# Moved work between waits, and a half-tile shift made by two on-chip transfers, in a three-pass fp32 layer kernel

## The chip, the cores and the metric

The kernel runs on one core of one Trainium2 chip. The metric is the device time of one execution in microseconds; the time before is the median of three runs. Engines are named as the hardware has them: TensorE (PE in the profile), VectorE (DVE), ScalarE (ACT), GpSimd (POOL), and SyncE (SP), which here only issues transfers.

## The reference, cut to what matters

One encoder layer on 1024 tokens of width 1024, in float32: a normalised input goes through one projection (1024 to 2304) whose columns feed three groups, their normalised outputs go through one output projection, and a squared-ReLU MLP of hidden width 4096 follows. The group that matters here is the chunked attention: four query heads, two key and value heads of 64, chunks of 64 tokens, and each chunk of queries reads its own chunk of keys and the one before.

```
def sliding_window_sink_attention(q, k, v, sinks, bias_band):
    ...
    def band(t):
        tc = t.reshape(B, nC, CHUNK, SWA_KV_HEADS, Dh)
        parts = [jnp.pad(tc, ((0, 0), (shift, 0), (0, 0), (0, 0), (0, 0)))[:, :nC]
                 for shift in reversed(range(WINDOW_CHUNKS))]
        return jnp.concatenate(parts, axis=2)
    kb, vb = band(k), band(v)
    ...
    o = jnp.einsum('bhgcqk,bckhd->bcqhgd', w.astype(vb.dtype), vb)
```

The two other groups are a stick-breaking attention (four heads of 64, strictly causal over all keys) and a recurrent block of width 512: a causal convolution over four tokens, two gates from small block-diagonal products, and a linear scan over the tokens, times a GeLU gate.

## The kernel before, in words

Every large product is made of three matmuls: both operands are split into a rounded high part and the rest (`w_hi`, `w_lo`, `act_hi`, `act_lo`), ScalarE writes the high part and VectorE the low one, and `three_passes` (L746, L748, L750) adds high times high, low times high and high times low in PSUM. Each engine has one program, written out in order; semaphores tie them together, and the order of the work is fixed by hand.

**Input projection.** The columns of `w_in` come in nine granules of 256 (`IN_COLS`), g = 0 to 8. SyncE's `load_in(g)` loads a granule as two halves into `stage` (L517); a half waits until VectorE has made the low part of the half that lay in `stage` before. ScalarE's `split_hi` rounds it (L1164), VectorE's `split_lo` subtracts (L1677). TensorE's `feature_major(g, n, half)` is one block of 24 matmuls, k = 0 to 7 with three passes each; blocks are counted as f = 4g + 2 half + n. Between blocks stand small pieces of work: after f = 4 `spread_norms` turns the token norms `rstd` into a row with eight transposes (L787), which ScalarE copies to `rs_row` and without which VectorE can copy no block out of PSUM; after f = 10, 16, 22 and 28 (`GATES_AFTER`) `gates(c)` makes the gate products of recurrent tile c (L819) once VectorE's `convolution(c)` is done (L1771). On `gates(c)` hang ScalarE's `recurrent(c)`, VectorE's `recurrent_input(c)` and `recurrent_scan(c)` (L1793 to L1798, which ends with `lru_done`), and after the last tile ScalarE's squares (L1305) and roundings (L1288) of the four recurrent tiles, VectorE's low parts of them (L1825), and then the softmax of the chunked attention.

**Chunked attention.** Four probability tiles h = 0 to 3. `window_scores(part)` (L847) makes scores for two tiles, VectorE's `window_max(h)` adds the bias and takes the maximum (L1870 to L1873), ScalarE's `window_exp(h)` follows (L1324), then VectorE's `window_norm(h)` (L1882), then TensorE's `window_turn(h)`, eight transposes (L911), then ScalarE's `window_copies(h)` (L1348). The values are turned token-major by `turn_cv` (L904), copied from PSUM to `cvtok` by ScalarE (L1317), and a second copy shifted by half a tile of 128 tokens, `cvshift`, is made by VectorE in `shift_v` (L1837 to L1840): the lower 64 partitions take the upper 64 of the tile before, the upper take the lower ones. `window_out(part, half)` (L939) reads `cvtok` for odd and `cvshift` for even chunks, and ScalarE's `window_output` copies it out (L1354).

**Around it.** `turn_v` transposes the values of the stick-breaking attention (L895), VectorE copies them to `vtok` (L1847); `recurrent_out(n)` is a row of twelve output-projection matmuls that needs nothing of the attentions; `scores(u)` (L958) are the stick-breaking scores, on which ScalarE's `weights` (L1366, L1370) wait, and of these `scores(1)` waits for the first two. TensorE's order before is

```
            window_turn(0)
            window_scores(1)
            window_turn(1)
            turn_cv()
            turn_v(0)
            window_out(0, 0)
            recurrent_out(0)
            window_out(0, 1)
            turn_v(1)
            scores(0)
```

ScalarE's order is `window_exp(0)`, `(1)`, `group_rsqrt(0)`, `window_copies(0)`, `(1)`, the copies to `cvtok`, `window_exp(2)`, `window_output(0, 0)`, `window_exp(3)`, `recurrent_row(0)`, `window_output(0, 1)`, `weights(0)`, `window_copies(2)`, `weights(1)`, `window_copies(3)`. VectorE's is `window_norm(1)`, `window_max(2)`, `group_rsqrt(0)`, `shift_v`, `window_max(3)`, `value_copies(0)`, `(1)`, `window_norm(2)`, `(3)`. SyncE issues, after the sink loads (L580), 16 small loads of gate weights (L586), then `load_in(2)` to `load_in(8)` and the output projection's granules; it issues in order and stops at each wait.

## Time and profile before

| | us |
|---|---|
| median of 3 runs (lowest, highest) | 1025.41 (1024.73, 1027.03) |
| the profiled execution, its own time | 1025.31 |
| its span, from first to last instruction | 1023.3 |
| TensorE busy in it | 1005.5 |
| VectorE, ScalarE, GpSimd busy | 796.3, 582.6, 90.8 |
| mean granted TensorE clock | 0.999 |

The span is what the profile shows; the run's time has about 2 us more around it. Starts and durations in the timeline are from the span's start. A wait is the idle time of an engine just before an instruction, put down to what ended it. After the first 350 us come the eight stages of the MLP, which the change does not touch.

### The profile page before, as it was taken

How to read it: one execution, taken by the hardware profiler on the slowest of the kernel's cores; microseconds unless marked ns; L12 is line 12 of the kernel's file. 1: busy time of each engine (PE TensorE's matmuls, PEld its weight loads, DVE VectorE, ACT ScalarE, POOL GpSimd, SP SyncE). 2: the span in 40 equal slices, each digit the busy share in tenths (PEclk: the TensorE clock that was granted, in tenths of full speed). 3: DMA queues.
4: the chain of work that ended last, by engine and by line, in shares of the span. 5: the costliest groups of instructions: out<-in, count | busy, mean ns of one | idle time of the engine just before them, and what ended most of it. 6: DMA issues, size and time to landing. Idle time of an engine off the chain costs nothing.

```text
span 1023.3 us, 12188 instructions
## 1 busy us (share of the span) xinstructions
PE 1005.5 (98%) x4846; PEld 812.4 (79%) x4846; DVE 796.3 (78%) x729; ACT 582.6 (57%) x760; POOL 90.8 (9%) x69
## 2 busy tenths in 40 slices
PE   9999999999999999999999999999999999999997
PEld 7878777877767788788888888888888888888884
DVE  6157759698787589967877777998777998778998
ACT  7424642759777547768653657333657333666455
POOL 0014213121322241000000000000000000000000
PEclk9999999999999999999999999999999999999999
DMA  9421111200101733021031031031031031035004
GB/s 331 138 83 42 42 42 42 83 1 1 42 2 42 265 126 144 1 103 63 1 114 51 1 121 45 1 123 42 1 124 42 1 124 42 1 124 206 0 1 165
DMA packets 38864, 74.64 MB, mean 73 GB/s; under 512 B 3444, under 2 KB 12952, under 8 KB 38808
## 3 DMA queue, kind: packets, MB, share of 16 engines
q1 hardware_dynamic: 38664, 73.83, 20.9%
q8 instruction: 39, 0.64, 0.3%
q14 instruction: 17, 0.14, 0.0%
q10 hardware_dynamic: 144, 0.03, 0.0%
HBM read 65.46 MB, written 8.39 MB: 72 GB/s over the span
## 4 chain that ended last, share of the span: by engine, by line
PE 86%; DVE 5%; ACT 3%; DMA 3%; SPq 2%; issue 1%; ACTq 0%; DVEq 0%
PE ps L746 26%; PE ps L750 26%; PE ps L748 26%; PE ps L983 2%; PE ps L911 2%; PE ps L958 2%; DMA xt<-in_x_turned 1%; DMA rel_row<-work 1%; SPq L586 1%; PE ps L819 1%; DVE y L2205 1%; DMA stage<-in_w_in 1%; PE ps L1058 1%; PE ps L828 1%; DVE out_gained L2143 0%
## 5 line engine op out<-in xcount | busy, mean ns | idle before, releaser
L746 PE MATMUL ps<-a_op,b_op 128*128 128x512 f32 x448 | 175.4, 392 | 2.5 <-issue 1.4
L750 PE MATMUL ps<-a_op,b_op 128*128 128x512 f32 x448 | 174.4, 389 | 0.0
L748 PE MATMUL ps<-a_op,b_op 128*128 128x512 f32 x448 | 174.3, 389 | 0.0
L746 PE MATMUL ps<-b_op,a_op 128*128 128x512 f32 x448 | 174.3, 389 | 0.0
L748 PE MATMUL ps<-b_op,a_op 128*128 128x512 f32 x448 | 174.3, 389 | 0.0
L750 PE MATMUL ps<-b_op,a_op 128*128 128x512 f32 x448 | 174.3, 389 | 0.0
L1524 ACT CAST a_op<-f 128x1024 fp32r<-128x1024 f32 x56 | 58.8, 1050 | 107.8 <-PE ps L750 77.7
L2049 DVE TENSOR_TENSOR b_op<-wq,b_op 128x1024 fp32r<-128x1024 f32 x96 | 117.0, 1219 | 0.0
L746 PE MATMUL ps<-act_hi,w_hi 128*128 128x512 f32 x288 | 113.6, 394 | 0.9 <-DVE w_lo L1677 0.7
L748 PE MATMUL ps<-act_lo,w_hi 128*128 128x512 f32 x288 | 112.1, 389 | 0.0
L750 PE MATMUL ps<-act_hi,w_lo 128*128 128x512 f32 x288 | 112.1, 389 | 0.0
L2038 DVE TENSOR_TENSOR a_op<-f,a_op 128x1024 fp32r<-128x1024 f32 x56 | 68.5, 1223 | 49.7 <-ACT a_op L1524 49.7
L1532 ACT CAST b_op<-wq 128x1024 fp32r<-128x1024 f32 x96 | 100.7, 1049 | 4.2 <-DVE y L1981 4.2
L746 PEld LDWEIGHTS ps<-a_op,b_op 128*128 128x128 f32 x448 | 84.1, 188 | 20.1 <-issue 1.8
L750 PEld LDWEIGHTS ps<-a_op,b_op 128*128 128x128 f32 x448 | 84.1, 188 | 17.6
L746 PEld LDWEIGHTS ps<-b_op,a_op 128*128 128x128 f32 x448 | 84.1, 188 | 17.5
L748 PEld LDWEIGHTS ps<-b_op,a_op 128*128 128x128 f32 x448 | 84.1, 188 | 17.5
L750 PEld LDWEIGHTS ps<-b_op,a_op 128*128 128x128 f32 x448 | 84.1, 188 | 17.4
L748 PEld LDWEIGHTS ps<-a_op,b_op 128*128 128x128 f32 x448 | 84.1, 188 | 17.0
L1524 ACT CAST a_op<-ut 128x1024 fp32r<-128x1024 f32 x32 | 33.6, 1052 | 74.4 <-PE ps L750 74.4
L746 PEld LDWEIGHTS ps<-act_hi,w_hi 128*128 128x128 f32 x288 | 54.2, 188 | 17.0 <-issue 3.4
L2092 DVE TENSOR_TENSOR y<-y,ps 128x1024 f32<-128x1024 f32 x54 | 63.1, 1215 | 0.0
(221 smaller groups left out, 1659.1 us busy)
## 6 DMA issues: line engine op xcount, KB each, us to landing
wq<-in_w_ff_in SPq DMA_DIRECT2D x16, 1024.0 KB, 5.4
wq<-in_w_ff_out SPq DMA_DIRECT2D x16, 1024.0 KB, 5.1
stage<-in_w_in SPq DMA_DIRECT2D x16, 512.0 KB, 4.0
y<-in_x SPq DMA_DIRECT2D x4, 1024.0 KB, 13.3
h_spill<-y SPq DMA_DIRECT2D x8, 512.0 KB, 2.7
h_back<-h_spill SPq DMA_DIRECT2D x2, 2048.0 KB, 12.0
out<-y SPq DMA_DIRECT2D x8, 512.0 KB, 3.2
stage<-in_w_out SPq DMA_DIRECT2D x6, 512.0 KB, 3.4
```

The costliest lines, as they stand in the source:

```text
L586: sp.dma_start(gate_w[r:r + HEAD, blk // 2, col:col + HEAD], w[0, blk])\
L746: nc.tensor.matmul(dst, stat[0], mov[0], start=first, stop=False, skip_group_check=chained)
L748: nc.tensor.matmul(dst, stat[0], mov[1], start=False, stop=False, skip_group_check=chained)
L750: return nc.tensor.matmul(dst, stat[1], mov[0], start=False, stop=last, skip_group_check=chained)
L911: mm = nc.tensor.transpose(ps[:, piece_bank(i), P * b:P * (b + 1)], c[:, P * b:P * (b + 1)], ident[:, :])
L958: mm = nc.tensor.matmul(ps[:, 2 * a + c, 0:cols.stop - cols.start], sq_t[p][rows, P * t:P * (t + 1)], sk_t[p][rows, cols], start=True, sto ...
L983: mm = nc.tensor.matmul(ps[HEAD * a:HEAD * (a + 1), 6, P * (t % 4):P * (t % 4 + 1)], vtok[:, j, P * p + HEAD * a:P * p + HEAD * (a + 1)], ...
L1524: nc.scalar.copy(a_op[:, (half + 2) % A_SLOTS, 0], src).then_inc(a_hi_ready, 1)
L1532: nc.scalar.copy(b_op[:, (half + 3) % B_SLOTS, 0], src).then_inc(b_hi_ready, 1)
L2038: nc.vector.tensor_tensor(slot[:, 1], a_source(*divmod(n, PRODUCTS), kk), slot[:, 0].bitcast(F32), ALU.subtract)\
L2049: nc.vector.tensor_tensor(slot[:, 1], src, slot[:, 0].bitcast(F32), ALU.subtract).then_inc(b_lo_ready, 1)
L2092: nc.vector.tensor_tensor(dst, dst, ps[:, bank:bank + 2, :], ALU.add)\
```

## The change

It has four parts. SyncE issues `load_in(2)` ahead of the 16 gate weight loads. TensorE's `spread_norms` moves from behind block 4 into block 5, after k = 2, and the last `gates` from behind block 28 into block 29, after k = 1. The two VectorE copies of `shift_v` become two transfers from `cvtok` to `cvshift` (229 KB and 262 KB, each to 64 partitions), issued by SyncE once `cvtok` is copied; VectorE keeps the memset of the first chunk, under a semaphore of its own. After `turn_cv` TensorE now goes to `recurrent_out(0)`, `window_out(0, 0)`, `turn_v(0)` in that order.

```diff
--- before.py
+++ after.py
@@ -240,8 +240,9 @@
         gelu_poly, gelu_sig, gelu_used = sem("gelu_poly"), sem("gelu_sig"), sem("gelu_used")
         decay_ready, one_minus, root_ready, lru_done = (
             sem("decay_ready"), sem("one_minus"), sem("root_ready"), sem("lru_done"))
-        v_turned, v_copied, cv_turned, cv_copied, cv_shifted = (
-            sem("v_turned"), sem("v_copied"), sem("cv_turned"), sem("cv_copied"), sem("cv_shifted"))
+        v_turned, v_copied, cv_turned, cv_copied, cv_shifted, cv_cleared = (
+            sem("v_turned"), sem("v_copied"), sem("cv_turned"), sem("cv_copied"),
+            sem("cv_shifted"), sem("cv_cleared"))
         win_scores, win_max, win_exp, win_probs = (
             sem("win_scores"), sem("win_max"), sem("win_exp"), sem("win_probs"))
         turned_ready, turned_copied = sem("turned_ready"), sem("turned_copied")
@@ -580,17 +581,22 @@
                 sp.dma_start(sink_c[HEAD * a:HEAD * (a + 1), kv:kv + 1],
                              swa_sinks[:, h:h + 1].partition_broadcast(HEAD))\
                     .then_inc(sinks_loaded, 16)
+            load_in(2, w_in[0], IN_COLS[2])
             for m, w in enumerate((lru_wa, lru_wx)):
                 for blk in range(2 * LRU_TILES):
                     r, col = HEAD * (blk % 2), HEAD * ((m + blk) % 2)
                     sp.dma_start(gate_w[r:r + HEAD, blk // 2, col:col + HEAD], w[0, blk])\
                         .then_inc(gate_w_loaded, 16)
 
-            for g in range(2, N_IN):
+            for g in range(3, N_IN):
                 load_in(g, w_in[0], IN_COLS[g])
 
             for n in range(2):
                 load_out(N_IN + n, w_out[0], (2 * P, 4 * P), 512 * n)
+            sp.wait_ge(cv_copied, 2)
+            sp.dma_start(cvshift[0:CHUNK, 1:TOK, :], cvtok[CHUNK:P, 0:TOK - 1, :])\
+                .then_inc(cv_shifted, 16)
+            sp.dma_start(cvshift[CHUNK:P, :, :], cvtok[0:CHUNK, :, :]).then_inc(cv_shifted, 16)
             load_out_by_group(N_IN + 2, w_out[0], 0)
             load_out_by_group(N_IN + 3, w_out[0], 512)
 
@@ -767,7 +773,7 @@
                         if k == KD - 1:
                             mm.then_inc(proj_ready, 1)
 
-            def feature_major(g, n, half):
+            def feature_major(g, n, half, between={}):
 
                 whi, wlo = w_slot(w_hi, g % 2, "in"), w_slot(w_lo, g % 2, "in")
                 for k in range(KD):
@@ -777,6 +783,8 @@
                                       (whi[:, k, cols], wlo[:, k, cols]),
                                       (act_hi[:, k, toks], act_lo[:, k, toks]),
                                       k == 0, k == KD - 1)
+                    if k in between:
+                        between[k]()
                 mm.then_inc(proj_ready, 1)
 
             def spread_norms():
@@ -868,15 +876,18 @@
                             pe.wait_ge(rs_row_ready, 1)
                         elif f >= 8:
                             pe.wait_ge(proj_copied, f - 7 if g == 2 else f - 3)
-                        feature_major(g, n, half)
-                        if f == 4:
-                            spread_norms()
+                        if f == 5:
+                            feature_major(g, n, half, {2: spread_norms})
+                        elif f == GATES_AFTER[-1] + 1:
+                            feature_major(g, n, half, {1: lambda: gates(LRU_TILES - 1)})
+                        else:
+                            feature_major(g, n, half)
                         if f == 8:
                             pe.wait_ge(proj_copied, 8)
                             pe.wait_ge(rel_back, 16)
                             nc.tensor.matmul(ps[:, 5, :], flip, work[0:CHUNK, 2, 0:4 * P],
                                              start=True, stop=True).then_inc(band_ready, 1)
-                        if 4 * g + 2 * half + n in GATES_AFTER:
+                        if 4 * g + 2 * half + n in GATES_AFTER[:-1]:
                             gates(GATES_AFTER.index(4 * g + 2 * half + n))
                         if f == 4 * N_IN - 4:
                             window_scores(0)
@@ -926,7 +937,8 @@
                 n = 2 * part + half
                 pe.wait_ge(turned_copied, win_piece(2 * part + 1, half) + 1)
                 if n == 0:
-                    pe.wait_ge(cv_shifted, 3)
+                    pe.wait_ge(cv_shifted, 32)
+                    pe.wait_ge(cv_cleared, 1)
                     pe.wait_ge(turned_copied, 4)
                 else:
                     pe.wait_ge(win_copied, n)
@@ -1011,9 +1023,9 @@
             window_scores(1)
             window_turn(1)
             turn_cv()
+            recurrent_out(0)
+            window_out(0, 0)
             turn_v(0)
-            window_out(0, 0)
-            recurrent_out(0)
             window_out(0, 1)
             turn_v(1)
             scores(0)
@@ -1834,11 +1846,7 @@
             def shift_v():
 
                 dve.wait_ge(cv_copied, 2)
-                nc.vector.memset(cvshift[0:CHUNK, 0, :], 0.0).then_inc(cv_shifted, 1)
-                nc.vector.tensor_copy(cvshift[0:CHUNK, 1:TOK, :], cvtok[CHUNK:P, 0:TOK - 1, :])\
-                    .then_inc(cv_shifted, 1)
-                nc.vector.tensor_copy(cvshift[CHUNK:P, :, :], cvtok[0:CHUNK, :, :])\
-                    .then_inc(cv_shifted, 1)
+                nc.vector.memset(cvshift[0:CHUNK, 0, :], 0.0).then_inc(cv_cleared, 1)
 
 
             def value_copies(part):
```

## Rows read from the trace of the kernel before

**Rows 1.** The page: the span, and the engines' busy time.
```profile
span 1023.3 us, 12188 instructions
...
PE 1005.5 (98%) x4846; PEld 812.4 (79%) x4846; DVE 796.3 (78%) x729; ACT 582.6 (57%) x760; POOL 90.8 (9%) x69
```

**Rows 2.** TensorE's waits, whole span: total us, times, longest us.
```profile
PE ps L895 <- ACT cvtok L1317: 1.2, 1, 1.2
...
PE ps L939 <- issue: 0.8, 1, 0.8
...
PE ps L746 <- DVE w_lo L1677: 0.7, 1, 0.7
PE ps L958 <- ACT sb_w L1370: 0.6, 1, 0.6
...
PE ps L787 <- DVE rstd L1692: 0.3, 1, 0.3
```

**Rows 3.** Timeline, 33 to 56 us: start us, us, what [idle before].
```profile
38.53 2.48 DVE L1807 SCALAR_TENSOR_TENSOR xr<-ps,rs_row 128x512 f32<-128x512 f32 x4 [2.34 <-ACT rs_row L1202]
...
40.10 5.07 SPq L586 DMA_DIRECT2D work<-in_lru_wx  x8
...
45.22 9.50 SPq L517 DMA_DIRECT2D stage<-in_w_in  x4
...
53.10 1.22 DVE L1677 TENSOR_TENSOR w_lo<-stage,w_hi 128x1024 fp32r<-128x1024 f32 x1 [1.47 <-ACT w_hi L1164]
```

**Rows 4.** Timelines by engine, 176 to 222 us.
```profile
177.15 1.99 PE L819 MATMUL ps<-work 64*128 64x512 f32 x8 [0.53 <-DVE work L1771]
...
195.72 2.01 ACT L1164 CAST w_hi<-stage 128x1024 fp32r<-128x1024 f32 x2 [3.73 <-PE ps L750]
...
196.12 1.22 DVE L1798 TENSOR_TENSOR xr<-xr,work 128x1024 f32<-128x1024 f32 x1
...
197.63 3.90 ACT L1305 ACTIVATE work<-xr 128x1024 f32<-128x1024 f32 x4
...
204.11 9.17 DVE L1825 SCALAR_TENSOR_TENSOR f_lo<-xr,columns_c,f_hi 128x1024 fp32r<-128x1024 f32 x4 [2.25 <-ACT f_hi L1288]
...
221.49 0.86 PEld L911 LDWEIGHTS ps<-ident,work 128*128 128x128 f32 x8 [0.41 <-DVE work L1882]
```

**Rows 5.** Timelines by engine, 226 to 237 us.
```profile
226.51 1.07 ACT L1317 COPY cvtok<-ps 128x512 f32<-128x512 f32 x2 [0.24 <-PE ps L904]
...
230.59 0.50 PE L746 MATMUL ps<-w_hi,f_hi 128*128 128x512 f32 x1
...
230.75 0.56 ACT L1354 COPY work<-ps 128x512 f32<-128x512 f32 x1
...
233.53 0.44 PE L939 MATMUL ps<-work,cvshift 128*64 128x128 f32 x4
...
235.69 1.29 DVE L1847 COPY vtok<-ps 128x512 f32<-128x512 f32 x2 [2.26 <-PE ps L895]
```

**Rows 6.** The chain that ended last, in order of time: start us, us, what.
```profile
228.12 0.62 DVE cvshift L1838
...
229.49 1.24 DVE sb_w L1870
...
232.27 1.22 ACT sb_w L1324 x6
...
242.91 1.77 PE ps L958 x8
```

**Rows 7.** Kinds of DMA issues: count, KB each, median us from issue to landing.
```profile
h_spill<-y SPq DMA_DIRECT2D x8, 512.0 KB, 2.7
...
stage<-in_w_out SPq DMA_DIRECT2D x4, 256.0 KB, 4.6
...
work<-in_lru_wa SPq DMA_DIRECT2D x8, 16.0 KB, 2.1
```

**Rows 8.** GB/s of all queues, 40 slices of 0.2 us from 322 us.
```profile
GB/s 0 0 0 102 123 133 317 369 410 389 430 297 72 215 154 143 246 266 348 358 287 287 195 72 41 20 20 20 10 0 0 0 0 0 0 0 0 0 0 0
```

## The prediction

> **What bounds the kernel now.** I read the page first. TensorE is busy for 1005.5 of 1023.3 us [rows 1], so nothing that only makes another engine shorter can pay; what can pay is TensorE's idle time, 17.8 us in all, some of it ahead of its first instruction and behind its last. The second view is the list of TensorE's waits. The ones that this change aims at are 0.7 us for the low half of the third weight granule, 0.3 us for the token norms, 1.2 us for `cvtok`, 0.8 us for `cvshift`, and 0.6 us for ScalarE ahead of `scores(1)` [rows 2]; a sixth, 0.53 us for the convolution ahead of the last `gates`, stands in [rows 4]. Together 4.1 us, 0.4% of the span: that is the most the change could bring if every wait went and none came back. So I followed each wait back in the timeline and in the chain that ended last, to see who is late next.
>
> **The third granule's load, moved ahead of the 16 gate weight loads: 0.7 us removed.** SyncE spends 0.63 us on each of them (5.07 for 8), the last ends at 45.2, and only then `load_in(2)` is issued; the low half of its second half runs from 53.10 to 54.32, and TensorE, which waits for it, starts 0.7 us late [rows 3, 2]. Issued 10.2 us earlier, the load is no longer the last thing: VectorE turns to it after four copies that end at 41.0 [rows 3], or near 43 with the next edit, still some 10 us ahead of TensorE. Its own waits are for granule 1's low halves, which TensorE reads already. Behind it the gate weights land 10.2 + 2.1 [rows 7] after their first issue, near 48, and the first `gates` comes three blocks after 54.3. What is queued behind on SyncE, `load_in(3)`, then waits for a low half that comes earlier too. Gain 0.7.
>
> **`spread_norms`, three k steps into the next block: 0.3 us removed.** The eight transposes start 0.29 us late, behind `rstd` [rows 2]. Nine matmuls of some 0.24 us (twelve stand between 230.59 and 233.53 [rows 5]) now lie ahead, so they start near 38 in place of 36.2. `rs_row` then comes at 40.2, and the next block that needs it starts near 42: covered. VectorE's four copies [rows 3] go from 38.5 to 40.3, with the slack just named. Gain 0.3; together 0.99 us with the granule.
>
> **The last `gates`, two k steps into block 29.** It waited 0.53 us [rows 4]. Six matmuls, 1.4 us, now go ahead of it. The convolution hangs by VectorE's and ScalarE's work on the `gates` before, so it comes 0.99 earlier; TensorE reaches `gates(3)` at 176.62 - 0.99 + 1.4 = 177.0, only 0.12 earlier than before (177.15), though TensorE itself is now 1.5 ahead. What hangs on `gates(3)` is a chain that TensorE doesn't enter: the sigmoids, the root, the scan, `lru_done` at 197.34, ScalarE's four squares at 197.63, its four roundings, VectorE's four low halves from 204.11 with no gap up to the first softmax, and at its end `window_turn(0)` at 221.5, whose weight load already waits on VectorE for 0.41 us [rows 4]. Before, the squares were held to 197.63 by ScalarE's `split_hi` ahead of them, which TensorE releases; that one now ends 1.5 earlier and `lru_done` (197.34 - 0.12, plus 0.05) takes over at 197.27. So the chain arrives 0.36 us earlier, not 1.5: **TensorE gets a new wait of about 1.1 us at `window_turn(0)`**, and of 1.5 us removed upstream 0.36 are left. If that chain had slack I don't see, up to 1.1 more would be left; if the move of `gates` cost more, nothing.
>
> **TensorE's new order after `turn_cv`.** `turn_cv` ends just ahead of the `cvtok` copies of 226.51 [rows 5], after the change near 226.1. `recurrent_out(0)` needs only things that are there, takes 2.94 [rows 5] and ends near 229.0; it covers the 1.2 us wait for `cvtok`. Then comes `window_out(0, 0)`, ahead of `turn_v(0)`, and it waits for the shifted values.
>
> **The shift as two transfers.** VectorE loses two copies, 1.37 us from 228.12 to 229.49, which are on the chain that ended last: they delay `window_max(3)`, whose end releases `window_exp(3)` at 232.27; from there ScalarE runs without a gap up to `scores(1)` at 242.91 [rows 6]. After, `window_max(3)` ends near 232.27 - 0.36 - 1.37 = 230.5. But the shift now takes: `cvtok` copied at 227.58 - 0.36 = 227.22 [rows 5]; SyncE, which has nothing due behind that wait until the next two output granules, issues the first at 227.25 and the second 0.64 later (the 0.63 of [rows 3], whose transfers also fill 64 partitions); then the landing of 229 KB and 262 KB. No transfer from SBUF to SBUF is in the trace. From below, a 16 KB one lands in 2.1 us. A 512 KB store out of SBUF takes 2.7; two of 256 KB to 64 partitions each, issued back to back, take 4.6 [rows 7], with other data ahead of them and a source in HBM. The pair moved at 143 to 246 GB/s at first and at 358 at most, against the 430 just before [rows 8]. I take 3.3 for the second: the store's 2.7 and a third of the way to the pair, as this source is near and its lines are long, but the partitions are half. It lands at 227.9 + 3.3 = 231.2, and `window_out(0, 0)` starts at 231.3, after a wait of 2.3 us that takes the place of 1.2 + 0.8.
>
> The Trainium skill on the same term, which the sum does not use: the page SBUF — State Buffer (section on Door 1, the DMA port swizzle) says that 64 partitions of one half reach 8 of the 16 ports; at half of its 436 GB/s the two would need 2.25 us of data, and with the fixed 2.0 us of the page DMA: Bandwidth & Descriptors (section on the anatomy of one DMA) land some 4.3 after the first issue, an estimate that gives +1.0 us in place of +0.7; the slow start of the pair in [rows 8] agrees with it.
>
> **Who waits for that.** ScalarE's order is unchanged: `window_exp(2)`, then the output copy of `window_out(0, 0)`, then `window_exp(3)`. So the copy, which before started at 230.75 [rows 5], now starts at 231.3 + 1.1 and `window_exp(3)` 0.55 later, at 232.95, where before it started at 232.27: **0.7 us later, and with it the chain of [rows 6]**, weights(0), weights(1) and `scores(1)`. VectorE: `turn_v(0)` now ends at 233.4, the value copies follow it and `turn_v(1)`, and end near 237.0, as before (236.98 [rows 5]), so it adds nothing. TensorE behind that: `turn_v(0)`, `window_out(0, 1)`, `turn_v(1)`, `scores(0)` fit before 237.5. From 243 on all engines follow one another by work and not by the clock, and the shift stays.
>
> **The sum.** Upstream -0.36; from `cvtok` to `window_exp(3)` +1.04; net +0.7 on the profiled 1025.31 (span 1023.3 and 2.0 around it). That execution lies 0.1 below the median of 1025.41. On the median: 1026.1. Each 0.1 us in the landing is 0.1 us of the kernel; break-even is a second transfer that lands 2.6 us after its issue.
>
> **Rivals.** *The transfers are quick.* At 2.1 us [rows 7] the second lands at 230.0, the sum is -0.6: 1024.8. At 2.7 it is +0.1. For it: SyncE has no other transfer under way, and SBUF is at both ends. Against: two transfers share the engines, and both are issued at 0.63. By that DMA page of the Trainium skill, 2.0 us and the second transfer's bytes at 436 GB/s make 2.6: break-even; it is a fit for another issue path, so I give it no more. *The transfers are as slow as the pair of [rows 7]*, the case on the other side: at 4.6 us it lands at 232.5, `window_exp(3)` starts at 234.25, +2.0: 1027.4; from 4.7 us it is slower by over 0.2%. For it: the one row of its shape. Against: that pair ran behind a 512 KB load. *The gap fillers' gain comes through:* the chain behind `gates(3)` has slack, no new wait at `window_turn(0)`, and 1.1 more is saved: -0.4 with my landing, 1025.0, and -1.7 with the quickest. For it: the waits list shows no wait of TensorE there; against: the 0.41 us of its weight load. *The change does nothing:* the waits only change their names; that is my case to within 0.7.
>
> **How the numbers follow.** My case (landing 2.9 to 3.9 us, +0.3 to +1.3) 0.5; quick 0.22; slow 0.13; the gain comes through 0.1; others 0.05, such as a lower clock after the longer gap (it is 0.999 in the mean now, but no gap of TensorE in [rows 2] is as long as 2.3 us). The range takes in the quick case with the gain (-1.7) and the slow one (+2.0, or +2.4 with no gain upstream): 1023.8 to 1027.9; my case alone is 1025.7 to 1026.7. About 0.2%, 2.05 us, is what a measurement tells from no change. Faster by more needs the quick landing and the whole upstream gain and a little besides: 0.07. Slower by more is the upper part of the slow case and a clock that falls: 0.12. Same: 0.81.
>
> **What the profile after would show.** TensorE's waits for `w_lo` near 54, for `rstd` near 36, for the convolution at 177 and for `cvtok` are gone; a wait of about 1.1 us stands at L911's first transposes, for VectorE; one of about 2.3 us for DMA at `window_out`; `scores(1)` waits near 1.2 in place of 0.6. Two issues of 0.6 us stand on SyncE at 227.25, and the second lands near 231.2. The prediction is wrong if `window_turn(0)` starts well before 221, or if `window_exp(3)` starts before 232 or after 234.

## The result and the profile after

The changed kernel took 1027.25 us (median of 20 runs, 1025.67 to 1028.77), the kernel before 1025.39 us (20 runs, 1024.14 to 1027.88). The ratio is 1.0014, 95% interval 1.0008 to 1.0020: slower by some 1.4 us, inside the 0.2% within which the prediction counted a time as the same. (The two medians differ by 1.86 us, more than the ratio says; its interval reaches from 0.8 to 2.05 us.) On the median that the forecast of 1026.1 was made on, 1025.41, the ratio makes 1026.8, just above its likeliest case's own range.

The page of the changed kernel: span and TensorE's busy time, which answer to [rows 1].

```profile
span 1025.5 us, 12189 instructions
...
PE 1005.9 (98%) x4846; PEld 813.4 (79%) x4846; DVE 794.6 (77%) x727; ACT 582.3 (57%) x760; POOL 93.4 (9%) x69
```

The span is 2.2 us longer, TensorE's busy time 0.4: the rest is idle time. Its waits over the whole span (total us, times, longest us) answer to [rows 2]:

```profile
PE ps L951 <- issue: 2.6, 1, 2.6
PE ps L752 <- DVE act_lo L1732: 1.6, 1, 1.6
...
PE ps L922 <- DVE work L1890: 1.1, 1, 1.1
...
PE ps L970 <- ACT sb_w L1382: 0.8, 1, 0.8
```

The five waits that the change aimed at (`cvtok`, `cvshift`'s copies, `w_lo`, `rstd`, the convolution at 177) are gone. In their place stand two that were not there, 2.6 us at `window_out(0, 0)` (L951; "issue" means that nothing the profile shows ended it, here the transfers) and 1.1 us at `window_turn(0)` (L922, for the normalised tile), and 0.8 in place of 0.6 at `scores(1)` (L970). The wait for `act_lo` (1.6) belongs to the first input tiles; in a second profile of the unchanged kernel, below, it is 1.8.

Timelines by engine, 33 to 50 us, beside [rows 3]: start us, us, what, and in brackets the idle time before.

```profile
34.25 1.14 SPq L518 DMA_DIRECT2D stage<-in_w_in  x2
...
38.77 1.04 PE L795 MATMUL ps<-ident,rstd 128*128 128x128 f32 x8
...
43.41 2.35 DVE L1689 TENSOR_TENSOR w_lo<-stage,w_hi 128x1024 fp32r<-128x1024 f32 x2
```

`load_in(2)` is now issued at 34.25, ahead of the gate weights; `spread_norms` starts with no wait (38.77); VectorE turns to the granule's low halves at 43.41, more than 10 us ahead of TensorE.

Timelines by engine, 176 to 222 us, beside [rows 4]:

```profile
177.36 1.99 PE L827 MATMUL ps<-work 64*128 64x512 f32 x8
...
197.59 3.90 ACT L1317 ACTIVATE work<-xr 128x1024 f32<-128x1024 f32 x4 [1.02 <-DVE xr L1810]
...
221.48 1.09 PE L922 MATMUL ps<-ident,work 128*128 128x128 f32 x8 [1.13 <-DVE work L1890]
```

`gates(3)` (L827) has no bracket any more. But ScalarE's squares (L1317) wait 1.02 us, for VectorE's scan, and TensorE stands 1.13 us ahead of `window_turn(0)`.

Timelines by engine, 226 to 235 us, beside [rows 5]:

```profile
226.49 1.07 ACT L1329 COPY cvtok<-ps 128x512 f32<-128x512 f32 x2 [0.23 <-PE ps L915]
...
227.59 0.50 SPq L597 DMA_DIRECT2D cvshift<-cvtok  x1
228.14 0.60 SPq L599 DMA_DIRECT2D cvshift<-cvtok  x1
...
231.96 0.70 PE L951 MATMUL ps<-work,cvshift 128*64 128x128 f32 x4 [2.56 <-issue]
...
233.98 0.59 ACT L1366 COPY work<-ps 128x512 f32<-128x512 f32 x1 [3.14 <-PE ps L951]
234.46 0.40 ACT L1336 ACTIVATE sb_w<-sb_w,m_row 128x128 f32<-128x128 f32 x1
```

SyncE issues 0.03 us after the `cvtok` copies end (227.56); the second transfer is issued at 228.14; TensorE comes out of its wait at 231.96. The kinds of DMA issues say how long they took (count, KB, median us from issue to landing), for [rows 7]:

```profile
cvshift<-cvtok SPq DMA_DIRECT2D x1, 256.0 KB, 3.7
cvshift<-cvtok SPq DMA_DIRECT2D x1, 224.0 KB, 2.9
```

The second lands at 228.14 + 3.7 = 231.84. And the chain that ended last, in order of time (start us, us, what), for [rows 6]:

```profile
229.40 2.56 issue
231.96 1.99 PE ps L951 x16
...
233.98 0.59 ACT work L1366
234.56 1.11 ACT sb_w L1336 x6
...
245.09 1.77 PE ps L970 x8
```

`window_exp(3)` (L1336) starts at 234.46, where it started at 232.27, and `scores(1)` at 245.09, where it started at 242.91. The same delay of 2.2 us at both, and it is the 2.2 us of the span.

One thing is in no row of before: the clock. First one window of the kernel before, then those of the changed kernel from 228 us; the columns are the stretch, its length, the busy time and count of PE, PEld, DVE, ACT and POOL, the granted clock, the DMA share and GB/s.

```profile
232.00:234.00 2.00, 2.00 (x16) 1.45 (x16) 1.42 (x3) 1.73 (x9) 0.00 (x0) 1.00 0.00 0
```

```profile
228.00:232.00 4.00, 1.44 (x9) 0.87 (x8) 2.60 (x4) 2.83 (x15) 0.00 (x0) 0.98 0.48 125
232.00:234.00 2.00, 2.00 (x17) 1.67 (x18) 0.00 (x0) 0.02 (x1) 0.00 (x0) 0.50 0.00 0
234.00:236.00 2.00, 2.00 (x16) 1.84 (x18) 0.33 (x1) 2.00 (x9) 0.00 (x0) 0.68 0.00 0
236.00:238.00 2.00, 2.00 (x22) 1.56 (x20) 1.24 (x3) 2.00 (x12) 0.00 (x0) 1.00 0.03 8
```

TensorE's granted clock is 0.50 of full, the lower of its two levels, from 231.8 to 235.3: 3.3 us of it behind the gap. `window_out(0, 0)` took 1.99 us there (chain, 231.96), where the same sixteen matmuls take 1.09 at full clock (in the filled gap, below). In before's profile no microsecond from 0 to 1021 has a clock under 0.98.

### The profile page after: what moved, and what is told of

Its sections match the earlier page's. It is cut to its first block, busy times and chain, and to the rows that moved or that the text cites. A ratio compares the mean times of both kernels' runs of the same rounds, so it can differ in the third digit from the quotient of the medians.

```text
span 1025.5 us, 12189 instructions
## 1 busy us (share of the span) xinstructions
PE 1005.9 (98%) x4846; PEld 813.4 (79%) x4846; DVE 794.6 (77%) x727; ACT 582.3 (57%) x760; POOL 93.4 (9%) x69
## 4 chain that ended last, share of the span: by engine, by line
PE 89%; DVE 5%; ACT 3%; issue 1%; DMA 1%; SPq 0%; DVEq 0%; ACTq 0%
PE ps L752 27%; PE ps L756 27%; PE ps L754 27%; PE ps L922 2%; PE ps L995 2%; PE ps L970 2%; DVE f_lo L1837 1%; PE ps L827 1%; DVE y L2213 1%; DMA xt<-in_x_turned 1%; PE ps L1070 1%; DVE out_gained L2151 0%; PE ps L951 0%; ACT sb_w L1382 0%; ACT work L1317 0%
## 6 DMA issues: line engine op xcount, KB each, us to landing
y<-in_x SPq DMA_DIRECT2D x4, 1024.0 KB, 12.5
```

## The experiments

The kernel start differs from execution to execution: TensorE's wait for the first input tiles lasts between 0.2 and 1.8 us. So stretches of the profiles are compared by distances. In the table, *a* is from TensorE's relative-bias matmul (at 18.89 us in before's profile, before all that the change touches) to the first transposes of `window_turn(0)`; *b* from the start of ScalarE's `cvtok` copies to the start of `window_exp(3)`; *c* from the same to `scores(1)`; *d* from the relative-bias matmul to `scores(1)`. Each is a difference of two starts in one kernel's timelines; from `window_turn(0)` to the `cvtok` copies it is 5.01 or 5.02 us in every kernel here.

| kernel | a | b | c | d | median us | ratio to before, 95% |
|---|---|---|---|---|---|---|
| before | 202.61 | 5.76 | 16.40 | 224.02 | | |
| before, a second time | 201.11 | 5.76 | 17.75 | 223.87 | 1026.33 | 0.9999 (0.9989 to 1.0010) |
| changed | 201.64 | 7.97 | 18.60 | 225.25 | 1027.25 | 1.0014 (1.0008 to 1.0020) |
| changed, a second time | 201.62 | 7.96 | 18.59 | 225.23 | 1026.80 | 1.0005 (0.9994 to 1.0015) |
| load and norms alone | 201.10 | 5.77 | 16.40 | 222.51 | 1024.59 | 0.9991 (0.9979 to 1.0003) |
| gates back | 201.08 | 7.16 | 18.25 | 224.34 | 1026.09 | 1.0000 (0.9987 to 1.0013) |
| copies back | 201.64 | 5.77 | 16.40 | 223.05 | 1024.98 | 0.9994 (0.9981 to 1.0007) |
| copies and gates back | 201.09 | 5.76 | 16.40 | 222.51 | 1024.14 | 0.9985 (0.9976 to 0.9994) |
| `turn_v` first | 201.62 | 7.09 | 18.06 | 224.70 | 1026.54 | 1.0005 (0.9993 to 1.0018) |
| half size | 201.63 | 6.19 | 16.82 | 223.46 | 1025.28 | 0.9997 (0.9982 to 1.0013) |
| filled gap | 201.63 | 7.09 | 17.72 | 224.36 | 1026.39 | 1.0008 (0.9999 to 1.0017) |
| late copies | 201.09 | 4.25 | 16.16 | 222.26 | 1024.50 | 0.9985 (0.9977 to 0.9994) |
| exp first | 201.09 | 4.25 | 16.15 | 222.26 | 1024.00 | 0.9981 (0.9972 to 0.9990) |
| weights early | 201.07 | 4.25 | 15.38 | 221.46 | 1023.24 | 0.9970 (0.9959 to 0.9981) |

The kernels below the first row were timed in three sets, each beside its own executions of before (medians 1025.72, 1026.11 and 1026.03), and the ratio is to those; the row "changed" is the result above. So times of different sets are compared by their ratios.

The distances are steady to some 0.03 us where nothing differs between two kernels (the 201.07 to 201.10 of six profiles), the timed ratios only to some 0.1%; so the distances carry the small differences, and the times say whether the end agrees. Two limits: each distance is from one execution, and all end at `scores(1)`. What is left of the span from there is 780.3 to 780.5 us in nine of the profiles, and 781.2 to 782.9 in gates back, copies back, copies and gates back, late copies and weights early, which have a stretch at the lower clock between 276 and 284 us; no distance shows that.

**The last `gates` back behind block 28.** All else is as in the changed kernel.

```diff
-                        elif f == GATES_AFTER[-1] + 1:
-                            feature_major(g, n, half, {1: lambda: gates(LRU_TILES - 1)})
...
-                        if 4 * g + 2 * half + n in GATES_AFTER[:-1]:
+                        if 4 * g + 2 * half + n in GATES_AFTER:
```

> The changed kernel, with the last gates back behind block 28. Theory: the move of gates did not save its 0.5 us but handed it on with a surcharge, since what waits for it is the chain through VectorE and ScalarE up to window_turn(0). Then with the move undone a wait of about 0.5 us comes back ahead of the last gates, the wait of 1.1 us at window_turn(0) shrinks to 0.5 or less, and window_turn(0) starts about 0.6 us earlier, counted from the first block; the kernel is 0.6 us faster than the changed one, 1026.6. Rival: the move is worth what it removed; then it is 0.5 us slower, 1027.8, with the wait at window_turn(0) as long as before.

The waits of TensorE in this kernel:

```profile
PE ps L949 <- issue: 2.6, 1, 2.6
...
PE ps L827 <- DVE work L1781: 0.5, 1, 0.5
```

The wait for the convolution is back with 0.5 us, the one at `window_turn(0)` is gone from the list, and *a* is 0.56 shorter. So the move of the last `gates` costs 0.56 us: the wait that it removed came back twice as long behind it, since the chain that hangs on `gates(3)` runs on ScalarE and VectorE alone. The gap at `window_out(0, 0)` is as in the changed kernel, 2.6. But *b* is 7.16 and not 7.97: the clock fell later. The windows of this kernel:

```profile
230.00:232.00 2.00, 1.32 (x17) 1.11 (x18) 0.00 (x0) 0.12 (x1) 0.00 (x0) 0.89 0.00 0
232.00:234.00 2.00, 2.00 (x12) 1.67 (x13) 0.22 (x1) 2.00 (x10) 0.00 (x0) 0.50 0.00 0
```

TensorE came out of the gap at 230.68 and did `window_out(0, 0)` at full clock; the fall came at 231.5, and most of its price stands in *c* (18.25). The time, 1026.09 with a ratio of 1.0000, lies below the expected 1026.6, and its interval tells it neither from before nor from the changed kernel: that the move costs 0.56 us rests on *a* alone.

**VectorE's copies back.** The two transfers are taken out, the two copies put in again; TensorE keeps its new order.

```diff
-            sp.wait_ge(cv_copied, 2)
-            sp.dma_start(cvshift[0:CHUNK, 1:TOK, :], ...
-            sp.dma_start(cvshift[CHUNK:P, :, :], ...
...
+                nc.vector.tensor_copy(cvshift[0:CHUNK, 1:TOK, :], cvtok[CHUNK:P, 0:TOK - 1, :])\
+                    .then_inc(cv_shifted, 1)
+                nc.vector.tensor_copy(cvshift[CHUNK:P, :, :], cvtok[0:CHUNK, :, :])\
+                    .then_inc(cv_shifted, 1)
```

> The changed kernel, with the shift made by VectorE's two copies again; TensorE's new order and the gap fillers stay. Theory: the loss lies in the late landing and in the lower clock that follows the gap of 2.6 us ahead of window_out. Then window_out(0, 0) waits 0.1 us or nothing, the granted clock stays at 1.00 there, window_exp(3) starts 2.5 us earlier than with the transfers, and the kernel takes 1024.8, below both. Rival: the new order of TensorE costs by itself (the value copies and turn_v come late); then it stays above 1026.

TensorE's waits:

```profile
PE ps L966 <- ACT sb_w L1378: 1.3, 1, 1.3
PE ps L918 <- DVE work L1890: 1.1, 1, 1.1
```

The 2.6 us gap is gone, *b* is back at 5.77, 2.20 shorter where 2.5 was expected, and the time goes with it: 1024.98, ratio 0.9994, against 1.0014 and 1.0005 of the changed kernel's two rows (the intervals of this one and the second overlap). The 1.1 at `window_turn(0)` stays, so the two parts are independent. At `scores(1)` stand 1.3 us: TensorE has caught up there, and waits for ScalarE's `weights`, whose distance (*c*) is that of before to 0.01. The transfers, then, cost 2.2 us in the changed kernel's profile, the clock's fall included (7.97 - 5.77). Behind that wait, the clock fell here too: in the chain that ended last, `scores(1)` takes 3.13 us, and 1.77 in [rows 6].

```profile
242.30 3.13 PE ps L966 x8
```

**The load and the norms alone**, on the kernel before, with nothing else of the change.

```diff
+            load_in(2, w_in[0], IN_COLS[2])
             for m, w in enumerate((lru_wa, lru_wx)):
...
-            for g in range(2, N_IN):
+            for g in range(3, N_IN):
...
-                        feature_major(g, n, half)
-                        if f == 4:
-                            spread_norms()
+                        feature_major(g, n, half, {2: spread_norms} if f == 5 else {})
```

> The kernel before, with the third granule's load ahead of the gate weights and with spread_norms inside block 5, and nothing else. Theory: these two waits come off for good, since the chain up to window_turn(0) begins at a block of TensorE that comes earlier with them; TensorE's later waits stay as they were. Then it is 1.0 to 1.3 us faster than before: 1024.3. Rival: they are handed on to window_turn(0) as the move of gates was; then a wait of 1 us stands there and the time is that of before, 1025.4 to 1025.7.

*a* is 1.51 us shorter than in before's profile, and the two start alike (the relative-bias matmul at 18.89 and 18.81); *b* and *c* are those of before: the two gap fillers bring 1.51, not 0.99. The waits list shows the 0.7 and 0.3 us that TensorE stood; it does not show what else the stop cost (below).

**The copies and the gates back**, both of the edits above: what is left is the load, the norms and TensorE's new order.

> The changed kernel, with VectorE's copies and the last gates where they were; the load, the norms and TensorE's new order stay. Theory: both losses are taken back and the gains stay: against the kernel with only the copies back (1024.98) it wins what the gates cost, 0.6 to 1.1 us, so 1024.1; the waits of 2.6 us at window_out and of 1.1 us at window_turn(0) are both gone. Rival: the new order gives nothing beyond the load and the norms; then it equals the kernel that has only those two.

In every distance it is the kernel with the load and the norms alone. The new order of TensorE gives nothing by itself: it removes waits for `cvtok` and `cvshift` (1.2 and 0.8), but `scores(1)` hangs on ScalarE's `weights`, and *c* is ScalarE's: TensorE only waits there longer, 1.3 in place of 0.6.

**`turn_v(0)` ahead of `window_out(0, 0)`.** TensorE's order becomes `recurrent_out(0)`, `turn_v(0)`, `window_out(0, 0)`, `window_out(0, 1)`, `turn_v(1)`, `scores(0)`: 1 us of its work goes into the gap.

> The changed kernel, with turn_v(0) ahead of window_out(0, 0) again (after recurrent_out(0)): nothing is taken away, but 1.0 us of other work fills the gap. Theory that the clock fell because of the length of the gap: the gap shrinks from 2.6 to about 1.5 us, the clock stays at 1.00 as it did past the gap of 1.2 us, window_out(0, 0) takes 1.0 in place of 2.0 us, window_exp(3) starts 1.0 us earlier, and the kernel gains 1.0 to 1.5 us: 1026.0. Rival: the lower clock has another cause (the mean load of the stretch); then it falls again and the kernel stays at 1027.2.

TensorE's timeline and the windows of this kernel:

```profile
231.78 0.44 PE L951 MATMUL ps<-work,cvshift 128*64 128x128 f32 x4 [1.70 <-issue]
...
233.65 0.44 PE L951 MATMUL ps<-work,cvshift 128*64 128x128 f32 x4 [0.77 <-ACT work L1366]
```

```profile
232.00:234.00 2.00, 1.23 (x23) 1.02 (x21) 0.00 (x0) 1.08 (x4) 0.00 (x0) 1.00 0.00 0
234.00:236.00 2.00, 2.00 (x18) 1.67 (x15) 0.00 (x0) 2.00 (x11) 0.00 (x0) 0.51 0.03 8
```

The gap falls to 1.70, `window_out(0, 0)` does not start earlier (231.78), but it runs at full clock, and *b* is 7.09 in place of 7.97: 0.88 us of the delay in *b* is the clock, 1.33 the transfers. The expectation that a gap of this length leaves the clock alone failed: it fell 2 us later, behind a further 0.77, so that *c* is still 18.06, and the time is 1026.54 where 1026.0 was expected.

**Half the size.** Four transfers, tiles 0 to 3 first and, once they have landed, 4 to 7; `window_out(0, 0)` waits for the first pair, `window_out(1, 0)` for the second.

```diff
-            sp.dma_start(cvshift[0:CHUNK, 1:TOK, :], cvtok[CHUNK:P, 0:TOK - 1, :])\
+            sp.dma_start(cvshift[0:CHUNK, 1:4, :], cvtok[CHUNK:P, 0:3, :]).then_inc(cv_shifted, 16)
+            sp.dma_start(cvshift[CHUNK:P, 0:4, :], cvtok[0:CHUNK, 0:4, :]).then_inc(cv_shifted, 16)
+            sp.wait_ge(cv_shifted, 32)
...
+                    if n == 2:
+                        pe.wait_ge(cv_shifted, 64)
```

> The changed kernel, with the shift in two pairs of transfers: tiles 0 to 3 first, which the first two window_out read, and tiles 4 to 7 after them. Theory that the landing is fixed cost and data: with half the bytes the second transfer of the first pair lands 0.5 to 0.6 us sooner (3.1 in place of 3.7 us from its issue), the gap shrinks to 2.0 us, and window_exp(3) starts 0.5 us earlier, or 1.5 if the clock stays up: 1026.7 or 1025.8. Rival: the landing is fixed cost alone; then it lands as late and nothing changes, 1027.2.

The DMA issues and TensorE's timeline of this kernel:

```profile
cvshift<-cvtok SPq DMA_DIRECT2D x3, 128.0 KB, 2.3
...
cvshift<-cvtok SPq DMA_DIRECT2D x1, 96.0 KB, 2.3
```

```profile
230.35 0.44 PE L957 MATMUL ps<-work,cvshift 128*64 128x128 f32 x4 [1.70 <-issue]
```

The transfer that TensorE waits for, the second of the first pair, was issued at 227.42, and SyncE, which waits for the same landing, goes on at 230.28: it took 2.8 us, where the one of 256 KB took 3.7. The gap is 1.70, *b* 6.19. A landing that cost the same at any size is out, and one that is all data too: halving it takes 0.9 us off, where 0.5 to 0.6 was expected, and as much off *b* (7.09 at full clock to 6.19). The clock stayed up there, and the time is 1025.28, where 1025.8 was expected for that case.

**A filled gap.** Twenty transposes of the identity, whose results nothing reads, stand between `recurrent_out(0)` and `window_out(0, 0)`; TensorE's real work comes no earlier.

```diff
             recurrent_out(0)
+            pe.wait_ge(cv_copied, 2)
+            for i in range(20):
+                nc.tensor.transpose(ps[:, 4, P * (i % 4):P * (i % 4 + 1)], ident[:, :],
+                                    ident[:, :])
             window_out(0, 0)
```

> The changed kernel with work added, none taken away: 20 transposes of the identity into a free bank (their result is not used), behind recurrent_out(0), once cvtok is copied; they fill some 2.2 of the 2.6 us in which TensorE waits for the transfers. Theory: the lower clock past the gap is a price of its own, beside the late landing. Then the transfers land as before, the clock stays at 1.00 from 232 to 236 us, window_out(0, 0) takes 1.0 in place of 2.0 us, window_exp(3) starts 1.0 us earlier, and the kernel is 1.0 to 1.7 us faster than the changed one, near 1025.9. Rival: the two halved stretches cost nothing that is not hidden, or the clock falls anyway; then it stays at 1027.2.

TensorE's timeline and the windows:

```profile
229.16 2.35 PE L1029 MATMUL ps<-ident 128*128 128x128 f32 x20
231.88 0.44 PE L951 MATMUL ps<-work,cvshift 128*64 128x128 f32 x4 [0.38 <-issue]
```

```profile
232.00:234.00 2.00, 2.00 (x26) 1.66 (x27) 0.00 (x0) 0.99 (x4) 0.00 (x0) 1.00 0.00 0
```

The clock stays at 1.00, and *b* is 7.09, as with `turn_v(0)` first. `window_out(0, 0)` starts 5.48 us behind the start of the `cvtok` copies, as late as in the changed kernel (5.47), and takes 1.09 us in place of 1.99: this is what the lower clock costs where it covers that stretch. That filling the gap keeps the clock up is not shown by it: this is one profile, 5 of the 11 timed executions still have a mean clock under 0.998 (7 of the 11 of the changed kernel beside them), and the median is 1026.39 against 1026.80, where 1025.9 was expected.

**Late copies and exp first.** Two kernels with `gates` back, in which the orders give the shift time: ScalarE runs `window_exp(3)` ahead of `window_output(0, 0)`, and TensorE's order is `recurrent_out(0)`, `turn_v(0)`, `scores(0)`, `window_out(0, 0)`, `turn_v(1)`, `window_out(0, 1)`. The one makes the shift by VectorE's copies, behind `window_max(3)`; the other by the two transfers.

```diff
             window_exp(2)
-            window_output(0, 0)
             window_exp(3)
+            window_output(0, 0)
```

> As the one before, with three moves more: VectorE makes the copies behind window_max(3), ScalarE runs window_exp(3) ahead of the output copy of window_out(0, 0), and TensorE puts turn_v(0) and scores(0) ahead of window_out(0, 0) and turn_v(1) ahead of window_out(0, 1). Theory: window_max(3) and then window_exp(3) end the wait of that stretch; with the shift off that chain window_exp(3) starts 1.4 us earlier than in the one before, and about 1.3 us more is gained: 1022.9 to 1023.5. Rival: VectorE is the next to be late (value copies and two norms follow); then it gains under 0.3 us.

> As the one before in every order, but with the shift made by the two transfers. Theory: the transfers are as good as the copies, or better, once something covers them: turn_v(0) and scores(0) stand ahead of window_out(0, 0), so that the landing, 4.2 us after cvtok is copied, ends 1 us or more ahead of need; no gap over 1 us and a clock of 1.00 there; VectorE is 1.4 us freer than with its copies, and the time is that of the one before or up to 0.7 us under it, 1022.5 to 1023.3. Rival: a cost of the transfers that is not the wait (slower neighbours, a longer landing); then it is slower than the one before by 0.5 us or more.

TensorE's waits at `scores` in the kernel with the transfers:

```profile
PE ps L968 <- ACT sb_w L1380: 1.3, 1, 1.3
...
PE ps L968 <- DVE m_row L1879: 0.5, 1, 0.5
```

No wait for the transfers is left; 0.5 us at `scores(0)` is for `window_max(3)`. Both have *b* 4.25, since `window_exp(3)` follows `window_exp(2)` with no gap, and *d* 222.26. So once both are covered, transfers and copies are worth the same, and both beat the kernel before. Both are slower than expected, though: 1024.50 and 1024.00, where 1022.9 to 1023.5 and 1022.5 to 1023.3 were expected. What *b* gained (1.5 us against before) did not all reach *c*, which fell by 0.25: ScalarE now stood ahead of `weights(0)`, for the copy of `window_out(0, 1)`. Its timeline in the kernel with late copies:

```profile
234.50 0.59 ACT L1360 COPY work<-ps 128x512 f32<-128x512 f32 x1 [0.69 <-PE ps L945]
```

**Weights early.** The kernel called exp first, with ScalarE's `weights(0)` ahead of `window_output(0, 1)`.

```diff
             recurrent_row(0)
-            window_output(0, 1)
             weights(0)
+            window_output(0, 1)
```

> The best version so far (transfers covered by turn_v(0) and scores(0), window_exp(3) first, last gates back), with ScalarE's weights(0) moved ahead of the output copy of window_out(0, 1), for which ScalarE waited 0.7 us. Theory: ScalarE is the last to be ready ahead of scores(1); then TensorE's wait there falls from 1.3 to 0.6 us and the kernel gains 0.5 to 0.7: 1023.4. Rival: VectorE's scan, which begins behind its second norm and not behind ScalarE, is what the next transposes wait for; then nothing is gained.

TensorE's wait at `scores(1)`:

```profile
PE ps L968 <- ACT sb_w L1380: 0.8, 1, 0.8
```

It falls from 1.3 to 0.8, *c* to 15.38 and *d* to 221.46: 2.56 less than before's profile, 1.05 less than with the load and the norms alone. The time is 1023.24 us, ratio 0.9970 (0.9959 to 0.9981), near the expected 1023.4 and better than both kernels. The wait was expected to fall to 0.6; *c* gained 0.77, a little more than the wait.

**Both kernels again.** The kernel before and the changed one, unchanged, each profiled and timed a second time.

> The changed kernel as it is, on the chip of these runs. My theory expects what the first profile showed: about 0.15% slower than before, 1.4 to 1.8 us; the second transfer landing 3.7 us after its issue, a gap of 2.6 us, a clock that falls behind it, and a wait of 1.1 us at window_turn(0). The rival, that the difference was one chip's, expects 1.000.

> The kernel before as it is, for a second profile of it. In the six profiles with the load moved, TensorE's first wait for act_lo lasted 0.7 to 1.8 us, in the one of before 0.24. Theory: that is the arrival of the first input tiles, which no part of the change touches, and it varies from run to run; then a wait of 0.2 to 1.8 us stands there and the ratio is 1.000. Rival: the change causes it; then it is near 0.2 again.

The changed kernel gave the same distances to 0.02 us. Its time, ratio 1.0005 (0.9994 to 1.0015), is less than the 0.15% expected, and by itself is not told apart from that of the kernel before. The kernel before did not repeat its distances: its first wait for `act_lo`, and its windows:

```profile
PE ps L746 <- DVE act_lo L1720: 1.8, 1, 1.8
```

```profile
230.00:232.00 2.00, 1.38 (x16) 1.30 (x16) 1.93 (x3) 1.91 (x11) 0.00 (x0) 0.74 0.02 4
232.00:234.00 2.00, 2.00 (x8) 1.50 (x5) 1.97 (x4) 1.26 (x4) 0.00 (x0) 0.50 0.00 0
234.00:236.00 2.00, 2.00 (x9) 1.46 (x7) 0.48 (x1) 2.00 (x12) 0.00 (x0) 0.90 0.00 0
```

In this execution the first tiles came late (1.8 us in place of 0.2), and there was no wait for `w_lo` or `rstd` later: *a* is 201.11, as if the load and the norms had been moved. (The clock was also at its lower level from 12.5 to 16.0 us there, so TensorE was later by 2.56 us at the start of *a*, and the loads had that much more time.) And the clock fell, behind gaps of 1.2 and 0.8 us, so that *c* is 17.75. By the mean granted clock of each timed execution, 70 of 103 of the kernel before (those timed beside the experiments) lay under 0.998, with medians 1.2 to 1.8 us above those of the others; of the changed kernel 25 of 31. So most executions of the kernel before pay for a lower clock too, and the profile of the first section was one that did not. The same grouping compares the two kernels with the clock held alike: at 0.998 or more, 1025.76 (6 executions of the changed kernel) against 1024.76 (33 of before); below it, 1027.25 (25) against 1026.28 (70). It is some 1.0 us in both.

## Why the prediction was right, and where not, by its steps

**The granule and the norms: direction right, size under-read.** Predicted 0.99, measured 1.51 in distance *a* (202.61 to 201.10). Both waits went. The sum took the idle time of TensorE's matmuls from the waits list; but in before's trace the weight loads (PEld) stood longer than the matmuls, 1.11 and 0.72 us at the two stops (54.38 and 36.23 us), 0.85 more together. That their restart is the missing 0.52 us is argued from that, and was not tried by itself. That the gain is not always there was not foreseen either: in an execution that starts late, the same distance is 201.11 with no edit at all. The timed gain of the two edits is 0.9 us, and its interval (0.9979 to 1.0003) reaches to nothing.

**The last `gates`: right.** A wait of about 1.1 us at `window_turn(0)` was predicted, 1.13 stands there; ScalarE's squares were to be held by `lru_done`, and they waited 1.02 us for just that. The prediction's terms make the move cost 0.63 (0.99 of gain upstream, 0.36 left); 0.54 to 0.56 was measured by undoing it. This part of the change is a loss.

**The two transfers: right in mechanism and sign, short in size.** Of the predicted +1.04 us from `cvtok` to `window_exp(3)`, *b* shows +1.33 at full clock (7.09 - 5.76). The term that was mis-sized is the landing: 3.3 predicted, 3.7 measured, less 0.09 because the second issue came 0.55 behind the first and not 0.64. The rest of that step, the output copy and `window_exp(3)` behind it, held: 1.65 us from `window_out(0, 0)` to `window_exp(3)` predicted, 1.61 in the filled gap (231.88 to 233.49). VectorE was not the one to wait for: `window_max(3)` ended at 230.67, where 230.5 was predicted, and had 3.8 us to spare. The small waits were read less well: `scores(1)` waits 0.8 us (1.0 in the second profile), where 1.2 was predicted; at full clock, in the filled gap, it is 1.3.

**The clock: a term left out of the sum.** The prediction named a lower clock after the longer gap among "others", 0.05, since before's profile had it at 0.999. It came, and cost 0.88 us of *b* in the profile (7.97 - 7.09; the filled gap shows the same work at full clock). What the changed kernel adds is less than that, because the kernel before pays for it as well in most of its executions.

**The prediction's own sign of being wrong.** It said that it would be wrong if `window_exp(3)` started after 234. It started at 234.46. Of that, 0.95 us is the late start of this execution: counted from the relative-bias matmul as in before's profile, it would be 233.51, inside the bounds (233.49 in the second profile), where 232.95 was predicted. So the sign fired on the number as it was written, and not on the number that the change accounts for.

**The sum.** Against the first profile of before: upstream -0.97 (*a*), transfers at full clock +1.33, clock +0.88, and 0.95 us by which TensorE started later, which is no part of the change: +2.19, the delay of `window_exp(3)`, `scores(1)` and the span. Without the start it is +1.24 (*d*, 225.25 - 224.02, to 0.01). Against the second profile, with its late start and lower clock, it is +1.38. The timed +1.4 lies by them, and so does the +1.0 of the executions grouped by clock; but single profiles of before differ by too much for more than that. That the forecast came so near is in part luck: the predicted +0.7 missed +1.24 by two errors of opposite sign: upstream -0.36 for -0.97, and from `cvtok` on +1.04 for +2.21; -0.61 and +1.17 make the 0.56. (A slip besides: by the prediction's own terms the quick landing of 2.1 us makes -0.5 and not -0.6; it changes nothing here.)

**The rivals.** *Quick transfers* fell: 3.7 us, with break-even at 2.6, and nothing that can be read as 2.1. *As slow as the pair of [rows 7]* (4.6) fell too, though its price was reached: with the clock, the stretch from `cvtok` cost 2.21, where this rival, its +1.98 and the 0.36 gained upstream, stood for +2.34. *The gap fillers' gain comes through* fell by its wait of 1.13 us. *The change only renames its waits* is true of TensorE's new order alone, shown by the kernel with copies and gates back.

Of the two rules of the Trainium skill that the prediction weighed, the port rule (page SBUF — State Buffer, section on Door 1, the DMA port swizzle) gave, with the fixed 2.0 us of the other, an estimate of 4.3 us from the first issue; the rows show 231.84 - 227.59 = 4.25. By it the sum would have been +1.0, the transfer term within 0.1 us. The trace agrees with its reason only in part: in the first slices of the view at the end, where by the issues one transfer moves alone or nearly so, the rate is up to 233 GB/s, a little above the 218 that are half of 436; later it rose to 348, so the two did not share 8 ports all the time. The 2.6 us for the second, which the prediction made from the 2.0 us and the full 436 GB/s of the Trainium skill's page DMA: Bandwidth & Descriptors (section on the anatomy of one DMA), disagree with the measured 3.7, and the measurement decides. It is the rate that fails there: the time outside the data, 2.2 us, is near that page's 2.0.

**What stays open.** What makes the granted clock fall was not settled. It fell around one gap of 2.56 us (0.2 us ahead of its end in the changed kernel, 0.5 ahead in the second profile, 0.8 behind it with gates back), behind 1.70 and 0.77 (`turn_v` first), behind 1.2 and 0.8 (before, second profile), and not behind 1.70 alone (half size), nor in the first profile of before, whose gaps were 1.2 and 0.8. With the copies back it fell behind 1.3 us at `scores(1)`, and not behind the same wait with exp first. With weights early it fell at 276.3 us, where TensorE's timeline has no wait from 240.61 to 279.81. So the length of a gap alone is no explanation, and a gap is not even needed. My theory that it was, with which the `turn_v` experiment was written, fell. Of the timed +1.4 us, the grouping by mean clock puts some 1.0 on differences other than how often the clock falls; how the rest divides, and what a fall costs in each kernel, the times don't tell.

## What to carry to other kernels

A piece of TensorE work put ahead of a small product fills a gap for less than it costs, when a chain of other engines hangs on that product and ends at TensorE again: follow the chain to its end before moving anything ahead of its head. A copy on an engine that is replaced by a transfer needs cover for the whole way, here 4.25 us from the source being ready to the second landing, in the orders of all engines at once; with that cover (ScalarE's next tile ahead of the output copy, and TensorE's `turn_v(0)` and `scores(0)` ahead of the product) it cost nothing against the copies, and without it 1.3 us at full clock and 2.2 where the clock fell at that place. And take a second profile of the kernel before, ahead of any sum in tenths of a microsecond: here two executions of the same program differed by 1.5 us in *a* and in the clock, and the forecast's term of 0.99 for the gap fillers holds only for one of them.

## What the runs showed of the hardware that was not expected

Two transfers from SBUF to SBUF, to 64 partitions each, issued 0.55 us apart, land 2.9 us (224 KB) and 3.7 us (256 KB) after their issues (these are the 229 and 262 KB of the prediction, in units of 1024); at 96 and 128 KB it is 2.3 in the median, 2.8 for the second of the first pair. The GB/s of all queues, in 40 slices of 0.2 us from 226 us, show the way of the pair in the changed kernel:

```profile
GB/s 0 0 41 0 0 0 0 0 0 0 0 0 0 125 197 233 233 108 251 307 348 328 328 0 0 20 20 0 0 0 0 0 0 0 0 0 0 0 0 0
```

The data moves from 228.6 to 230.6, at 246 GB/s in the mean of the ten slices (2.0 us); 1.0 us passes ahead of it from the first issue, and 1.2 behind it until the landing is seen. So of 4.25 us less than half is data.

The clock's lower level came in the midst of a kernel whose TensorE is 98% busy, in most executions of an unchanged program, and in the middle of the profiles for some 3 to 4 us each time, at different places: around 231 us, at 242, at 276 to 284, once at 12.5. It cost 0.88 us of *b* in the changed kernel, next to nothing of *b* with gates back behind the same gap (7.16 against 7.09), and 1.35 us of *c* in the second profile of the kernel before (17.75 - 16.40, with *b* the same).
